# A hybrid decoder layer on one core: three buffers for pairs of experts, the ple gate weights loaded last, e scaled where it is drained, decay rows spread by bf16 matmuls

## The chip, the core and the metric

The kernel runs on one NeuronCore of a Trainium2 chip. The time is the device time of one execution in microseconds (us). Engines are named as in the profile: PE (TensorE matmuls), PEld (its weight loads), DVE (VectorE), ACT (ScalarE), POOL (GpSimd), SP (SyncE, which issues DMAs). The host does nothing but pass the arrays.

## What is computed

One decoder layer over 256 tokens of width 1024, all in float32:

```python
xn = rms_norm(h, norm_mix);  proj = xn @ w_in
# mixer 1: causal conv + silu, gated delta rule over chunks (8 heads x 128), decays exp(g_t - g_s)
# mixer 2: softmax attention with forget gates (16 heads x 64): s + c_t - c_s, causal
h = h + (sigmoid(gate_a) * y_a + sigmoid(gate_f) * y_f) @ w_out
# 64 experts, top 8, hidden 256, plus one shared expert
hn = rms_norm(h, norm_ffn)
routed = sum over e of (silu(hn @ we_gate[e]) * (hn @ we_up[e]) * gate[:, e]) @ we_down[e]
h = h + routed + (silu(hn @ ws_gate) * (hn @ ws_up)) @ ws_down
# per-layer input embedding
e = rms_norm(p @ w_ple, ple_norm)
g = sigmoid(rms_norm(h, ple_gate_norm) @ w_ple_gate)
out = h + g * e
```

The weights of the 64 experts are 3.1 MB each in float32, 201 MB in all; every other input together is some 60 MB.

## The kernel before

Each engine has its own program, and semaphores order them. The 256 tokens are two tiles of 128 (n = 0, 1). PSUM has eight banks; up to the expert loop, `bank_fills()` lists every use of a bank, which go round the eight in that order. PE waits for a bank's last reader (`open_bank`), the reader waits for the fill (`wait_filled`), and other steps wait for it to be drained (`wait_drained`). A big arena of SBUF is cut by hand, and its parts are used again in later stages.

**Mixers.** A tile of 512 columns of a weight matrix (2 MB) is projected for both token tiles by `project` (L722, eight matmuls of 128x512 in float32, which the profile shows as 16 records). Between the projections of mixer 2's columns PE fills `gb.j` and `bb.j` (L784): rows of g and beta of 16 heads and chunks, spread over all 128 partitions. For that DVE copies the transposed g and beta (`gbT`) out, POOL writes a block diagonal array from it with `affine_select` (`gd`, `bd`, 16 partitions x 2048), and PE multiplies it by ones: one float32 matmul with 16 rows and 512 columns for each j of 4 and each of the two kinds. `cb.j` (L893, eight of them) spreads the cumulated forget gates of mixer 2 in the same way, from `cd` (16 x 4096), which POOL writes once `o1.0` and `o1.1` are filled.

**Embedding.** PE computes p @ w_ple in four pieces `e.n.j` (L971). ACT copies each to `e_t` (L546). Behind the shared expert's silu ACT squares and sums `e_t` (L666, written to `hn` as a dump), then copies the transposed hidden of the shared expert (L669), on which PE's second matmul of that expert (L1028) waits. POOL makes the root. DVE scales `e_t` by the root and by `ple_norm` (L1516, L1517) in front of its expert loop; at the end it multiplies by the gate (L1557) and adds h (L1558).

**Experts.** A loop takes two experts (a pair) at a time, 32 pairs. A token tile gives each expert up to 32 slots (a second pass over all pairs would run if an expert had more; here one pass runs). For a pair PE does: gate and up products (L1075, 64 records), the adding of the former pair's output to the tokens (L1053), two transposes (L1082), the gathering of the next pair's tokens by one-hot bf16 matmuls (L1041, 48), two small ones (L1046, L1047), and the down product (L1093, 32 records). A pair's weights are 6.29 MB: gate and up 2.1 MB each, down 2.1 MB. They go to one of **two** buffers (`pair_at`, `gu_in`, `d_in`), each loaded by three DMAs on SP (`load_pair`, L408 and L411): gate and up once PE has done L1075 of the pair that had the buffer, down once PE has done its L1093. Pair 0 is loaded when the transposed mixture is drained, pair 1 when `wo.1.1` is filled, both ahead of the loop. The weights of the ple gate (`wpg`, 4.2 MB, used by L1117 behind the loop) have memory of their own and are loaded by two DMAs on ACT's queue (L678) just ahead of ACT's loop. PE's, DVE's and SP's loops have a body of two pairs.

## Time and profile before

| | |
|---|---|
| median of 3 runs | 1047.62 us (1047.4 to 1049.5) |
| profiled execution, whole | 1047.64 us |
| its span, first to last instruction | 1045.9 us |
| TensorE clock granted, mean | 0.998 |
| PE busy, share of the span | 1001.6 us, 96% |
| DVE, ACT, POOL busy | 315.3, 205.6, 61.7 us |
| moved by DMA | 264.41 MB, mean 253 GB/s |
| chain that ended last | PE 62%, DMA 32%, DVE 3% |

The profile's busy time of PE is modelled at its end, so 96% does not say that PE is never waiting. The stages by the span's time: up to 106 us convolution and its projections; to 204 the projections of mixer 2 with `gb` and `bb`; to 310 the triangular inverse; to 358 merge gates with `cb`; to 429 attention; to 530 output projection, router, shared expert; 530 to 1008 the expert loop; then the ple gate and the store.

### The profile page before, as it was taken

The page shows a single profiled execution, that of the slowest core. Times are in us where ns is not written, and L with a number is a line of the kernel's source. Part 1 is how long each engine was busy: PE and PEld are TensorE (multiplying, and loading weights), DVE is VectorE, ACT ScalarE, POOL GpSimd, SP SyncE. Part 2 cuts the span into 40 slices and gives each one's busy share as a digit, 9 for nine tenths or more (in the row PEclk, how much of TensorE's full clock was granted, in tenths as well). Part 3 has the DMA queues.
Part 4 walks back from the last instruction along what each step waited for, and adds up shares of the span by engine and source line. Part 5 has one row for each costly group of instructions (what it writes and reads, how often), then busy time and mean ns, then how long its engine had stood idle before and what let it go on. Part 6 is the DMA issues. An engine that isn't in the chain of part 4 may idle for free.

```text
span 1045.9 us, 17182 instructions
## 1 busy us (share of the span) xinstructions
PE 1001.6 (96%) x7371; PEld 519.8 (50%) x7371; DVE 315.3 (30%) x691; ACT 205.6 (20%) x407; POOL 61.7 (6%) x84
## 2 busy tenths in 40 slices
PE   6999999999999999999999999999999999999998
PEld 5888443579874555444743333333333333333343
DVE  2555802266636334112521111111111111111122
ACT  1200201215330563111301111111111111111111
POOL 5000600000052000000000000000000000000000
PEclk9999999999999999999999999999999999999999
DMA  7633342420022242656459999999999999999911
GB/s 226 236 139 138 125 161 81 161 81 1 1 81 80 81 154 88 232 186 246 190 192 414 421 421 421 421 421 421 421 420 421 420 421 421 421 421 421 421 42 41
DMA packets 60338, 264.41 MB, mean 253 GB/s; under 512 B 5921, under 2 KB 8338, under 8 KB 35346
## 3 DMA queue, kind: packets, MB, share of 16 engines
q1 hardware_dynamic: 58226, 259.77, 62.2%
q10 hardware_dynamic: 2080, 4.19, 1.1%
q8 instruction: 22, 0.36, 0.1%
q14 instruction: 10, 0.08, 0.0%
HBM read 262.91 MB, written 1.05 MB: 252 GB/s over the span
## 4 chain that ended last, share of the span: by engine, by line
PE 62%; DMA 32%; DVE 3%; ACT 1%; issue 1%; SPq 1%; POOL 0%; DVEq 0%; ACTq 0%; POOLq 0%
DMA arena<-in_we_up 31%; PE bank L722 23%; PE bank L1075 12%; PE bank L750 8%; PE bank L807 5%; PE bank L715 3%; PE bank L1117 3%; PE bank L1008 1%; ACT arena L546 1%; PE bank L1028 1%; PE bank L784 1%; PE bank L893 1%; SPq L408 1%; PE bank L874 1%; PE bank L1093 1%
## 5 line engine op out<-in xcount | busy, mean ns | idle before, releaser
L1075 PE MATMUL bank<-arena 128*32 128x512 f32 x2048 | 226.3, 593 | 17.9 <-DMA arena<-in_we_up 16.8
L722 PE MATMUL bank<-arena,actT 128*128 128x512 f32 x384 | 169.3, 596 | 0.0
L1075 PEld LDWEIGHTS bank<-arena 128*32 128x32 f32 x2048 | 69.7, 110 | 173.3 <-issue 154.4
L546 ACT ACTIVATE arena<-bank 128x512 f32<-128x512 f32 (+2 forms) x132 | 70.7, 571 | 247.0 <-PE bank L722 154.7
L722 PEld LDWEIGHTS bank<-arena,actT 128*128 128x128 f32 x384 | 71.4, 190 | 91.1 <-issue 90.3
L1093 PE MATMUL bank<-arena 128*32 128x512 f32 x1024 | 116.5, 595 | 0.0
L722 PE MATMUL bank<-arena 128*128 128x512 f32 x192 | 83.9, 595 | 2.0 <-ACT arena L546 2.0
L750 PE MATMUL bank<-actT,arena 128*128 128x256 f32 x384 | 83.8, 380 | 1.6 <-DVE actT L1156 1.6
L1526 DVE SCALAR_TENSOR_TENSOR arena<-arena,gslot,bank 128x256 f32<-128x256 f32 x32 | 15.4, 481 | 230.2 <-ACT arena L685 230.2
L750 PEld LDWEIGHTS bank<-actT,arena 128*128 128x128 f32 x384 | 72.6, 190 | 11.7 <-issue 2.0
L685 ACT ACTIVATE arena<-bank 128x256 f32<-128x256 f32 x32 | 12.3, 383 | 278.6 <-PE bank L1075 278.6
L1053 PE MATMUL bank<-arena 64*128 64x512 f32 x256 | 63.6, 615 | 0.0
L807 PE MATMUL bank<-arena 128*128 128x128 f32 x512 | 59.5, 275 | 1.3 <-ACT arena L546 1.3
L1093 PEld LDWEIGHTS bank<-arena 128*32 128x32 f32 x1024 | 30.0, 109 | 59.2 <-issue 57.4
L807 PEld LDWEIGHTS bank<-arena 128*128 128x128 f32 x512 | 58.3, 192 | 1.9 <-issue 1.9
L722 PEld LDWEIGHTS bank<-arena 128*128 128x128 f32 x192 | 36.0, 190 | 46.1 <-issue 46.1
L715 PE MATMUL bank<-ident,arena 128*128 128x128 f32 x333 | 44.4, 281 | 11.0 <-DVE arena L1145 7.4
L1041 PE MATMUL bank<-onehot,arena 128*128 128x64 bf16 x1584 | 51.6, 193 | 0.0
L1041 PEld LDWEIGHTS bank<-onehot,arena 128*128 128x128 bf16 x1584 | 50.7, 98 | 0.9 <-issue 0.6
L715 PEld LDWEIGHTS bank<-ident,arena 128*128 128x128 f32 x333 | 39.0, 145 | 20.7 <-issue 17.5
L1529 DVE COPY arena<-bank 128x512 f32<-128x512 f32 x32 | 22.1, 692 | 88.5 <-PE bank L1041 88.5
L1538 DVE COPY arena<-bank 128x512 f32<-128x512 f32 x32 | 22.1, 692 | 77.7 <-PE bank L1093 77.7
(226 smaller groups left out, 709.4 us busy)
## 6 DMA issues: line engine op xcount, KB each, us to landing
arena<-in_we_gate SPq DMA_DIRECT2D x32, 2048.0 KB, 17.4
arena<-in_we_up SPq DMA_DIRECT2D x32, 2048.0 KB, 21.9
arena<-in_we_down SPq DMA_DIRECT2D x32, 2048.0 KB, 20.2
arena<-in_w_in SPq DMA_DIRECT2D x17, 2048.0 KB, 7.6
arena<-in_w_branch_gdn SPq DMA_DIRECT2D x2, 2048.0 KB, 9.2
arena<-in_w_branch_fox SPq DMA_DIRECT2D x2, 2048.0 KB, 8.0
arena<-in_w_out SPq DMA_DIRECT2D x2, 2048.0 KB, 7.8
arena<-in_w_ple_gate ACTq DMA_DIRECT2D x2, 2048.0 KB, 22.3
```

The costliest lines, as they stand in the source:

```text
L546: a.activation(dst, ps(name)[:, 0:cols_used] if len(dst.shape) == 2 else ps(name)[:, 0:cols_used].rearrange("p (a b) -> p a b", a=dst.shap ...
L715: ins = t.transpose(o[0:w, i * P:i * P + rows_in], v, ident[0:rows_in, 0:rows_in])
L722: ins = t.matmul(o[:, :], lhs[:, c, n * P:n * P + P], w[:, c, :], start=(c == 0), stop=(c == KC - 1))
L750: ins = t.matmul(o[:, i * S:i * S + S], w[:, c, col:col + P], actT[:, c, :], start=(c == 0), stop=(c == KC - 1))
L807: ins = t.matmul(o[:, i * P:i * P + P], lhs(b), rhs(b), start=True, stop=True)
L1041: ins = t.matmul(bank[5 + half][:, c * P + n * 2 * CAP:c * P + (n + 1) * 2 * CAP], hparts[:, k, n, (4 * half + c) * P:(4 * half + c + 1) * P],
L1053: ins = t.matmul(bank[2 * n + j][:, :], spread[s][hp, :], y[hp, WT * j:WT * j + WT], start=False, stop=False, skip_group_check=True)
L1075: ins = t.matmul(bank[4][i * CAP:i * CAP + CAP, :], xg[:, c, i * CAP:i * CAP + CAP], w, start=(c == 0), stop=(c == KC - 1))
L1093: ins = t.matmul(bank[4 + j][i * CAP:i * CAP + CAP, :], hidT[:, c, i * CAP:i * CAP + CAP], d_in[s][:, i % 2, c * D + WT * j:c * D + WT * j ...
L1117: ins = t.matmul(bank[4 + NT * j + n][:, :], actT[:, c, n * P:n * P + P], wpg[j][:, c, :], start=(c == 0), stop=(c == KC - 1))
L1529: v.tensor_copy(xg[:, 4:8, :], bank[6][:, :].rearrange("p (c s) -> p c s", c=4)).then_inc(xb_ready, 1)
L1538: v.tensor_copy(y[:, WT:D], bank[5][:, :]).then_inc(y_ready[1], 1)
```

## The change

**A ring of three.** `SLOTS = 3`, `pair_at = [24576, 12288, 0]`. To fit a third buffer in the arena, other things move: the shared expert's weights and hidden, `hn`, `ple_norm` and the output tile into the down part of a buffer, `spread` into `actT`, and `wpg` into the gate and up part of buffer 2. SP's loads ahead of the loop are in another order (the `...` below `mT` is the shared expert's gate and up weights), and `wpg` is loaded by SP last, once PE has done L1075 thirty times (`passes` holds the 30 for one pass), the last time for pair 29. The loops of PE, DVE and SP have a body of three pairs; on PE and DVE the first and the last pair stand outside, on SP the last two loads.

```diff
-        pair_at = [PAIR_WORDS, 0]
+        pair_at = [24576, 12288, 0]
...
-        wpg = [at(WPG + i * KC * WT, KC * WT).rearrange("p (c n) -> p c n", c=KC) for i in range(2)]
+        wpg = [at(pair_at[2] + i * KC * WT, KC * WT).rearrange("p (c n) -> p c n", c=KC) for i in range(2)]
...
+            load_gate_up(0, slice(0, 2))
+            wait_filled(sp, "yf.1.1")
             sp.dma_start(ngain, norm_ffn.to_broadcast([P, D])).then_inc(ngain_loaded, 16)
+            for n in range(NT):
+                wait_drained(sp, f"mT.{n}.1")
...
+            load_gate_up(1, slice(2, 4))
+            wait_filled(sp, "wo.0.1")
+            load_gate_up(2, slice(4, 6))
             wait_filled(sp, "wo.1.0")
             wait_filled(sp, "wo.1.1")
+            sp.dma_start(sdw, ws_down[0].rearrange("(q c) d -> q c d", c=2)).then_inc(sdw_loaded, 16)
+            wait_filled(sp, "sh.0")
+            wait_filled(sp, "sh.1")
+            load_down(1, slice(2, 4))
+            for n in range(NT):
+                for j in range(2):
+                    wait_drained(sp, f"e.{n}.{j}")
+            sp.wait_ge(parts_ready, 2 * NT)
+            load_down(0, slice(0, 2))
+            sp.wait_ge(shared_done, 1)
+            load_down(2, slice(4, 6))
+            with sp.Fori(0, PAIRS // SLOTS - 1) as k:
+                for s in range(SLOTS):
+                    load_pair(s, bass.ds(k * 6 + (6 + 2 * s), 2), k * SLOTS + (s + 1))
+            for i in range(PAIRS // SLOTS * SLOTS, PAIRS):
+                load_pair(i % SLOTS, slice(2 * i, 2 * i + 2), i - SLOTS + 1)
...
+            sp.wait_ge(pgu_filled, sp.value_load(passes[0:1, 2:3], min_val=PAIRS - 2, max_val=PAIRS * (P // CAP) - 2))
+            for j in range(2):
+                sp.dma_start(wpg[j], w_ple_gate[0].rearrange("(c q) n -> q c n", q=P)[:, :, WT * j:WT * j + WT]).then_inc(wpg_loaded, 16)
```

**e at its drain.** ACT squares and sums `e.n.j` straight from PSUM (four of 512, each into a column of its own), DVE drains the bank as it multiplies by `ple_norm`, and the root is applied at the end in the multiplication by the gate. L666, L1516 and L1517 are gone.

```diff
-                drain(f"e.{n}.{j}", e_t[:, n, WT * j:WT * j + WT])
+                a.activation(ejunk, ps(f"e.{n}.{j}")[:, :], ACT.Square, accum_out=e_ss[:, 2 * n + j:2 * n + j + 1]).then_inc(ess, 1)
...
+                close(v.tensor_tensor(e_t[:, n, WT * j:WT * j + WT], ps(nm)[:, :], plen[:, WT * j:WT * j + WT], ALU.mult), nm)
...
-                    seq(v.tensor_tensor(o, o, e_t[:, n, WT * j:WT * j + WT], ALU.mult))
+                    seq(v.scalar_tensor_tensor(out=o, in0=e_t[:, n, WT * j:WT * j + WT], scalar=e_ri[:, n:n + 1], in1=o, op0=ALU.mult, op1=ALU.mult))
```

**Rows spread in bf16.** DVE splits g, beta and the forget sums into three bf16 parts (four small operations each time), PE transposes the 48 rows in bf16, and each head's row is spread by a bf16 matmul of 48 rows whose weights are a column of a constant `pick`, repeated 128 times. POOL's three `affine_select` and the waits on them are gone.

```diff
-                close(t.matmul(o[:, :], ones[0:16, :], src[0:16, 4 * int(j):4 * int(j) + 4, :], start=True, stop=True), name)
+                for i in range(4):
+                    ins = t.matmul(o[:, i * P:i * P + P], bc(pick[:, 4 * int(j) + i], 1, P), row, start=True, stop=True)
+                close(ins, name)
...
-                    close(t.matmul(o[:, :], ones[0:16, :], cd[0:16, 2 * j:2 * j + 2, :], start=True, stop=True), f"cb.{j}")
+                    for i in range(2):
+                        ins = t.matmul(o[:, i * S:i * S + S], bc(pick[:, 2 * j + i], 1, P), cT3, start=True, stop=True)
+                    close(ins, f"cb.{j}")
```

How the instructions stand in a row, at three places. First SP, from the last tile of w_out to the loop, before (`filled`, `drained` with a number are banks; `pgu_filled` counts L1075, `y1_filled` L1093):

```order
L378 DMA arena<-in_w_out 128x8x512 [waits filled0]
L408 DMA arena<-in_we_gate 128x2x2048 [waits drained1,drained7]
L408 DMA arena<-in_we_up 128x2x2048
L411 DMA arena<-in_we_down 128x2x2048
L417 DMA arena<-in_ws_down 128x2048
L421 DMA arena<-in_ple_norm 128x1024 [waits filled5,filled4]
L423 UNCONDITIONAL_BRANCH
L408 ISA [waits pgu_filled]
L411 DMA arena<-in_we_down 128x2x2048 [waits y1_filled]
```

and now:

```order
L383 DMA arena<-in_w_out 128x8x512 [waits filled0]
L409 DMA arena<-in_we_gate 128x2x2048
L409 DMA arena<-in_we_up 128x2x2048
L422 DMA arena<-in_norm_ffn 128x1024 [waits filled2]
L425 DMA arena<-in_ws_gate 128x2048 [waits drained1,drained7]
L426 DMA arena<-in_ws_up 128x2048
L409 DMA arena<-in_we_gate 128x2x2048 [waits filled3]
L432 DMA arena<-in_ws_down 128x2048 [waits filled5,filled4]
L412 DMA arena<-in_we_down 128x2x2048 [waits filled7,filled6]
L412 DMA arena<-in_we_down 128x2x2048 [waits drained4,drained7,parts_ready,drained6,drained5]
L412 DMA arena<-in_we_down 128x2x2048 [waits shared_done]
L444 UNCONDITIONAL_BRANCH
```

Gate and up of pair 0 now stand directly behind w_out's tile, those of pairs 1 and 2 ahead of the shared expert's down weights, and the three down loads between the shared expert and the loop.

Second, PE among the projections of mixer 2, before:

```order
L722 MATMUL bank<-arena,actT 128x512 x32
L784 MATMUL bank<-arena,ones 128x512
L722 MATMUL bank<-arena,actT 128x512 x8
...
L797 MATMUL bank<-ident,stat 16x128 x2
L715 MATMUL bank<-ident,arena 128x128 x32
```

and now (L750 is the projection, L814 the spreading, L743 the transpose `cT`):

```order
L750 MATMUL bank<-arena,actT 128x512 x32
L814 MATMUL bank<-stat,pick 128x128 x4
L750 MATMUL bank<-arena,actT 128x512 x8
...
L743 MATMUL bank<-identb,cf 48x128 x2
L737 MATMUL bank<-ident,arena 128x128 x32
```

Where one float32 matmul of 512 columns stood, four bf16 ones of 128 stand; nothing else moved there.

Third, ACT between the shared expert's silu and the expert loop, before (the rows with `shared_done` and the one behind it are the ple gate's weights):

```order
L661 ACTIVATE arena<-bank 128x256 [waits filled7]
L666 ACTIVATE arena,e_ss<-arena 128x1024 [waits drained6,drained5,parts_ready]
L666 ACTIVATE arena,e_ss<-arena 128x1024 [waits drained4,drained7]
L669 ACTIVATE arena<-bank 128x256 [waits hidT_filled] x2
L672 ACTIVATE arena<-bank 128x512 [waits xa_filled]
L678 DMA arena<-in_w_ple_gate 128x8x512 [waits e_ready,shared_done]
L678 DMA arena<-in_w_ple_gate 128x8x512
```

Now the two L666 and the two DMAs are gone from ACT, and the DMAs stand on SP behind the last pair:

```order
L460 TENSOR_LOAD passes
L460 ISA x2
L462 DMA arena<-in_w_ple_gate 128x8x512 x2
L466 DMA out<-arena 128x512 x4
```

## Rows read from the trace of the kernel before

**Rows 1.** The page's part 2: GB/s in 40 equal slices of the span

```profile
GB/s 226 236 139 138 125 161 81 161 81 1 1 81 80 81 154 88 232 186 246 190 192 414 421 421 421 421 421 421 421 420 421 420 421 421 421 421 421 421 42 41
```

**Rows 2.** The chain that ended last, in time: start us, us, what

```profile
552.93 21.58 DMA arena<-in_we_up
```

**Rows 3.** Timeline of PE in the expert loop: start, us, what, [idle before <-releaser]

```profile
530.56 7.07 PE L1075 MATMUL bank<-arena 128*32 128x512 f32 x64 [1.10 <-DVE arena L1504]
...
544.77 7.05 PE L1075 MATMUL bank<-arena 128*32 128x512 f32 x64
...
558.96 7.05 PE L1075 MATMUL bank<-arena 128*32 128x512 f32 x64
...
574.56 7.07 PE L1075 MATMUL bank<-arena 128*32 128x512 f32 x64 [1.23 <-DMA arena<-in_we_up]
...
604.46 7.07 PE L1075 MATMUL bank<-arena 128*32 128x512 f32 x64 [0.29 <-DMA arena<-in_we_up]
...
993.15 7.07 PE L1075 MATMUL bank<-arena 128*32 128x512 f32 x64 [0.29 <-DMA arena<-in_we_up]
...
1013.62 27.70 PE L1117 MATMUL bank<-arena,actT 128*128 128x512 f32 x64 [0.20 <-DVE actT L1552]
```

**Rows 4.** Busy time by stretch: PE, PEld, DVE, ACT, POOL, clock, DMA share, GB/s

```profile
510.00:535.00 25.00, 22.07 (x148) 13.11 (x150) 13.76 (x34) 3.60 (x8) 1.48 (x4) 0.93 0.00 1
...
560.00:980.00 420.00, 403.51 (x4376) 155.95 (x4372) 67.45 (x196) 54.89 (x112) 0.00 (x0) 1.00 1.01 421
```

**Rows 5.** Timelines of ACT's and SP's DMA issues around the loop's start

```profile
534.96 1.06 ACTq L678 DMA_DIRECT2D arena<-in_w_ple_gate  x2
...
537.86 0.39 SPq L408 DMA_DIRECT2D arena<-in_we_gate  x1
538.34 0.45 SPq L408 DMA_DIRECT2D arena<-in_we_up  x1
```

**Rows 6.** DMA issues from 0 to 530 us: KB each, median us to landing

```profile
arena<-in_we_up SPq DMA_DIRECT2D x2, 2048.0 KB, 13.4
```

**Rows 7.** Timeline of PE among mixer 2's projections, with gb (L784)

```profile
114.12 27.63 PE L722 MATMUL bank<-arena,actT 128*128 128x512 f32 x64
141.69 1.12 PE L784 MATMUL bank<-arena,ones 16*128 16x512 f32 x2
142.74 7.13 PE L722 MATMUL bank<-arena,actT 128*128 128x512 f32 x16
149.80 1.12 PE L784 MATMUL bank<-arena,ones 16*128 16x512 f32 x2
```

**Rows 8.** Timeline of PE among the merge gates, with cb (L893)

```profile
324.80 7.13 PE L722 MATMUL bank<-arena,actT 128*128 128x512 f32 x16
...
333.77 7.13 PE L722 MATMUL bank<-arena,actT 128*128 128x512 f32 x16
```

**Rows 9.** Timeline of PE in the first pair: the bf16 matmuls

```profile
539.75 1.56 PE L1041 MATMUL bank<-onehot,arena 128*128 128x64 bf16 x48
541.15 0.22 PE L1046 MATMUL bank<-identb,onehot 128*128 128x128 bf16 x1
...
541.31 3.64 PE L1093 MATMUL bank<-arena 128*32 128x512 f32 x32
```

**Rows 10.** Timeline of all engines from the router to the shared expert's second product

```profile
502.76 0.23 DVE L1436 TENSOR_TENSOR wsm<-wsm,rbias 128x64 f32<-128x64 f32 x1 [6.73 <-ACT wsm L546]
...
517.55 0.19 ACT L666 ACTIVATION_READ_ACCUMULATOR arena<-arena 128x1 f32 x1
...
518.19 0.29 DVE L1471 TENSOR_REDUCE gsum<-bank 128x1 f32<-128x128 f32 x1
...
519.20 8.80 PE L1028 MATMUL bank<-arena 128*128 128x512 f32 x16 [1.26 <-ACT arena L669]
```

**Rows 11.** The DMA queues from 560 to 980 us, all of them: packets, MB, share

```profile
q1 hardware_dynamic: 22833, 176.04, 100.9%
q10 hardware_dynamic: 332, 0.65, 0.4%
```

300 lines of the change are left out of this document (161 added, 139 removed).

## The prediction

> **What bounds the kernel now.** I first read the rate of the transfers over the span [rows 1]: the first half of the span moves 100 to 250 GB/s and the expert loop stands at 420 to 421 for as long as it runs. A rate that flat says that DMA is full there; the chain of waits agrees, since from 553 us on each second step of it is a load of `we_up` of 21.6 us or a little more [rows 2], 31% of the span in all. Then I read the starts of L1075 in PE's timeline [rows 3]. Pairs 0, 1 and 2 start at 530.56, 544.77 and 558.96, two steps of 14.20 us with no wait: that is PE's own time for a pair. From pair 3 (574.56) each start waits for `we_up`; from pair 3 to pair 5 (604.46) it is 29.90 us, so 14.95 us a pair, and the last, pair 31, starts at 993.15 = 574.56 + 28 x 14.95. A pair is 6.29 MB, and 6.29 MB / 14.95 us = 421 GB/s, the rate of the stretch [rows 4]. So the loop is bound by DMA, but only by 0.75 us in 15; PE's "busy" hides that. In contrast, from 510 to 535 us DMA moves 1 GB/s [rows 4]: both buffers are full, and nothing can be fetched. And the ple gate's 4.2 MB are fetched at 534.96, just in front of the first load of the loop (537.86) [rows 5], though L1117 wants them at 1013.62.
>
> **Part 1: the ring of three and the gate weights last.** Before the loop the change fetches one pair more, 14.95 us of DMA, into idle DMA time, and takes 4.2 MB (9.96 us at 421 GB/s) out of the loop's way. Together 24.9 us less lies in front of the last pair. PE can use only what brings it down to its own time. PE's floor: pair 31 starts at 530.56 + 31 x 14.20 = 970.76 instead of 993.15, which is 22.4 us earlier. DMA's floor: the loop's first load is issued at 537.86 as now (PE's first L1075 frees a buffer), but it is pair 3's. Up to the landing of pair 31's gate and up come 28 whole pairs and 9.96 us: 28 x 14.95 + 9.96 = 428.6 us, plus what a load costs beyond its bytes. For that I have two values. The two `we_up` loads ahead of the loop land 13.4 us after their issue [rows 6], some 0.48 us behind the gate's; 13.4 + 0.48 - 9.96 = 3.9. In the present loop, from the issue at 534.96 to pair 3's landing at 574.5 come 4.19 + 6.29 + 4.19 = 14.7 MB, 34.9 us, so 4.7. DMA's floor is thus 970.4 to 971.2, against 970.76 for PE: a margin of +0.4 to -0.4 us. The first pairs have slack (24.9 us at the start, which shrinks by 0.75 a pair), so it is only the last pair or two that may wait. I take 0.4 us of loss: **gain 22.0 us**. If the loop starts earlier for other reasons, both floors move with it, since the first load waits for PE.
>
> Are the earlier loads in time? Pair 0's down is now issued behind the shared expert's gate and up products (some 516 us in the old time), behind pair 1's down: two of 4.98 us and 3.9, so 530, wanted at 541.31 [rows 9]. Pair 2's down, behind L1028 (528), lands near 537, wanted 24 us later. The shared expert's down weights, wanted at 519.20 [rows 10], go out at 490 with nothing before them in the queue. Early in the loop the queue must not run dry: pair 3's 14.95 us of data begin some 2 us behind 537.86 and last to about 555; pair 4 is issued at PE's second end of L1075 (552), 1 us to spare after the same start-up. The gate weights wait for the thirtieth L1075 and stand behind pair 31's down: 971 + 4.98 + 9.96 = 986, plus nothing new for start-up; L1117 wants them at 1013.62 - 22.4 = 991. Cover of 5 us; if it is gone, each us is paid in full.
>
> **Part 2: rows spread in bf16.** Plain projections take 27.63 us for four, between starts 27.57, so 6.89 each [rows 7]. From one `gb` to the next are 149.80 - 141.69 = 8.11 us, so one costs 1.22; of that 2 of 16 records of a projection, 0.86, are columns, and 0.36 is the change of tile shape. Two `cb` with a projection take 333.77 - 324.80 = 8.97 [rows 8], so 2.08 for the two, 1.72 of columns and 0.36. PE has no gap on either side (106 to 204 us, 310 to 358), so what is saved moves everything behind it; DVE, which reads the banks, is idle most of that time. New price: 48 bf16 matmuls of 64 columns and two small ones take 541.31 - 539.75 = 1.56 us [rows 9], at most 0.0325 each, so 0.065 for 128 columns and 0.26 for the 512 of a `gb` or `cb`. Saved: 0.60 each, 16 times, **9.6 us**; I take 9.5, since the bf16 ones have their weights changed four times. The worst near row is 0.22 for a lone bf16 transpose of 128 columns [rows 9]: four of them would cost 0.88 and save nothing on the eight `gb` and `bb`, two cost 0.44 and save 0.42 on each `cb`: 3.4 us in all. The best, the columns for nothing, is 13.8. Nearest in kind is the row of 48, also a chain of different weights. The shape's 0.36 I leave, as 48 rows are still not the whole array. The two transposes `gbT` and `cT` in bf16: 0.1 us each. DVE's eight small splitting operations (0.2 us each) fall among the convolutions, where PE sets the pace; DVE is busy 30% of the span. POOL's selects ran beside PE's work: nothing.
>
> The Trainium skill ("TensorE: Matmul & The Clock Gate", section "Wait — 56ns, not 53.3ns?") gives 55.6 ns from start to start of bf16 matmuls of 128 columns at full clock. By it a `gb` costs 0.22 instead of 0.26, and part 2 would come to an estimated 10.2 us.
>
> **Part 3: e.** ACT's two L666 stood in front of L669, for which PE's L1028 waited until 519.20 [rows 10]. Without them the next that is late is DVE's L1471 (518.19 + 0.29 = 518.48), as L1028 also waits for the rank bank to be drained: gain 0.7 us. ACT's square of `e.0.0` stands in front of the four drains that PE waits for ahead of `wo`, and reading the sum adds up to 0.19 [rows 10]: loss 0.2. DVE's four new drains are 0.7 each, three of them in the 6.7 us of idle ahead of the router's 502.76 [rows 10]. The scaling that left DVE's first pair (4 us) was beside L1075: nothing. The last multiplication has the same 512 elements: nothing.
>
> **Sum.** 22.0 + 9.5 + 0.2 + 0.7 - 0.2 = 32.2 us. The profiled execution took 1047.64, 1.7 more than its span of 1045.9, and is within 0.1 of the median, so the forecast is 1047.6 - 32.2 = **1015.4 us**.
>
> **Rivals.**
> (a) *DMA stays the limit.* The floors are equal to 0.4 us, so every us of late or missing feed (the queue dry once in pairs 3 to 5, the gate's 2 KB pieces) is paid. For it: the start-up values differ by 0.8, and the reserve of the first pairs is about 1 us. Price 2 to 6 us, time 1017 to 1021.5.
> (b) *The spreading saves little*, as weights repeated from one column load slowly, or the change of shape is paid per matmul. No row of before has such weights. Price 3 to 6 us, time 1018.5 to 1021.5.
> (c) *Better than forecast*: columns nearly free and a cheaper change of shape, 1011 to 1013.5.
> (d) *Slower than before.* PE's loop body grows from two pairs to three, from 2 x 316 to 3 x 316 loads and matmuls. From 560 to 980 us only the two data queues move anything [rows 11], none for instructions, so the body of two stays in the engine through 14 turns. If the body of three did not, each of ten turns would fetch code through the full DMA engines. It decides above 32.2 / 10 = 3.2 us a turn. A load costs 3.9 us beyond its bytes (above), so with one such wait a turn the time is 1015.4 + 39 = 1054; behind a whole pair in the queue it would be 15 us a turn, 1165. Against it: the body grows by half only, and the chain shows no cost at the present turn (pair 1 to pair 2, 14.19).
> The Trainium skill ("Runtime: NRT & Kernel Launch", section "Instruction fetch mechanics") says that a taken branch out of the present window forces a fetch, which speaks against any loop; it also gives PE room for 2048 instructions, by which a body of some 950 stays, as the trace shows for 632.
> (e) *The ring is not filled*, because a moved load waits for something late: pair 2's gate and up then come 9.96 later, the time 1024.
>
> **How the numbers follow.** Forecast, 1013.5 to 1017: 0.58. (a) 0.13, (b) 0.11, (c) 0.08, (d) 0.04, (e) 0.03; something between 1025 and 1045, 0.03. From 1012 to 1021 lie the forecast, nearly all of (a) and (b) and half of (c), 0.58 + 0.12 + 0.10 + 0.04 = 0.84; a narrower range would cut into the bounds of the two start-up values and of the bf16 price. A measurement of this kernel tells about 0.2% (2 us) from no change. Faster: all but (d) and a hundredth, 0.94; same 0.02; slower 0.04.
>
> **What would show it.** In the changed trace: L1075 starts every 14.2 us to the end, with waits for `we_up` only in the last pairs, 440 us from the first to the last; 6.89 + about 0.62 from one `gb` to the next and 6.89 + about 0.88 with two `cb`; L1028 starting with DVE's release of the rank bank and no longer with L669; L1117 not waiting for its weights; DMA busy from 443 us on in pieces; no instruction packets within the loop. I am wrong in part 1 if steps of 14.95 come back from the middle on, in part 2 if a `gb` still costs 1 us, and in all if a step of PE at a turn of the loop is longer than at the others.

## The result, and the profile after

The changed kernel takes **1011.4 us** (median of 4 runs, 1011.35 to 1011.56) against 1047.9 for the kernel before (median of 4, 1047.4 to 1049.5); the ratio is 0.965, with a 95% interval of 0.963 to 0.967. The forecast was 1015.4 with a range from 1012 to 1021: the direction was right and nine tenths of the gain were foreseen (32.2 of 36.2 us, counted from the forecast's 1047.6), but the time is 4.0 us below the forecast and 0.6 us outside the range. The profiled execution took 1011.35 us with a span of 1009.6 (before: 1047.64 and 1045.9), so its span is 36.3 us shorter. All working below is on these two spans.

The page of the changed kernel first: the GB/s of the 40 slices, and the chain of waits by engine and by line.

```profile
GB/s 229 228 123 148 140 123 155 167 61 24 1 84 83 84 117 134 156 294 392 42 319 420 418 422 423 422 422 422 422 422 422 422 422 422 422 421 423 420 165 42
...
q8 instruction: 26, 0.43, 0.2%
...
PE 62%; DVE 1%; ACT 1%; issue 1%; POOL 0%; DVEq 0%; ACTq 0%
PE bank L1102 22%; PE bank L1120 11%; PE bank L750 10%; PE bank L1084 6%; PE bank L1072 5%; PE bank L1152 3%; PE bank L1039 1%; PE bank L1109 1%; PE bank L1059 1%; PE bank L983 1%; ACT arena L572 1%; PE bank L737 1%; PE bank L1002 0%; PE bank L1031 0%; PE bank L961 0%
```

DMA is still full in the loop (418 to 423 GB/s), as in [rows 1]. But it has gone from the chain, where the kernel before had a load of `we_up` in each second step [rows 2]: full and binding are two things. The timeline of PE shows which it is. Here are the first two pairs, and the last two with the product behind the loop (columns as in [rows 3]; L1102 is the old L1075, L1152 the old L1117):

```profile
516.97 7.07 PE L1102 MATMUL bank<-arena 128*32 128x512 f32 x64 [0.86 <-DVE arena L1561]
...
531.18 2.33 PE L1102 MATMUL bank<-arena 128*32 128x512 f32 x20
...
942.60 7.05 PE L1102 MATMUL bank<-arena 128*32 128x512 f32 x64
...
956.78 7.06 PE L1102 MATMUL bank<-arena 128*32 128x512 f32 x64
...
977.24 3.24 PE L1152 MATMUL bank<-arena,actT 128*128 128x512 f32 x7 [0.20 <-DVE actT L1607]
```

From pair 0 to pair 31 it is 439.81 us, 31 steps of 14.19 on average; none of the starts behind pair 0 has a wait in brackets. Before it was 462.59 [rows 3]. PE's waits from 500 us to the end, by line and releaser (total, times, longest), hold no transfer at all:

```profile
PE bank L1102 <- DVE arena L1561: 0.9, 1, 0.9
PE bank L1138 <- issue: 0.9, 1, 0.9
PE bank L1145 <- DVE h L1602: 0.7, 1, 0.7
PE bank L1059 <- DVE gsum L1527: 0.7, 1, 0.7
PE bank L1051 <- DVE arena L1519: 0.6, 1, 0.6
PE bank L1152 <- DVE actT L1607: 0.2, 1, 0.2
```

It was close, though. Here are the last pair's `we_up` and the ple gate weights in the timeline of SP's queue (start and length of the issue), and then the view of the transfers for the issues from 921 to 928 us (last column: us from issue to landing):

```profile
921.33 1.93 SPq L409 DMA_DIRECT2D arena<-in_we_gate  x1
923.30 4.62 SPq L409 DMA_DIRECT2D arena<-in_we_up  x1
...
935.52 22.84 SPq L462 DMA_DIRECT2D arena<-in_w_ple_gate  x2
```

```profile
arena<-in_we_up SPq DMA_DIRECT2D x1, 2048.0 KB, 33.2
```

923.30 + 33.2 = 956.5, and pair 31 starts at 956.78. A `we_up` that landed 13.4 us after its issue with only the gate weights ahead of it [rows 6] now takes 33 us behind a full queue and still comes 0.3 us before it is wanted. The other signs of part 1 hold too: the last instruction packets of the loop move before 600 us, and none from there to 940.

The spreading, in PE's timeline, with a `gb` (L814) and the two `cb` (L923) between projections (L750):

```profile
141.62 0.39 PE L814 MATMUL bank<-stat,pick 48*128 48x128 bf16 x4
141.95 7.13 PE L750 MATMUL bank<-arena,actT 128*128 128x512 f32 x16
149.01 0.40 PE L814 MATMUL bank<-stat,pick 48*128 48x128 bf16 x4
...
325.33 0.61 PE L923 MATMUL bank<-stat,pick 48*128 48x256 bf16 x4
325.87 7.13 PE L750 MATMUL bank<-arena,actT 128*128 128x512 f32 x16
332.94 0.61 PE L923 MATMUL bank<-stat,pick 48*128 48x256 bf16 x4
```

149.01 - 141.62 = 7.39, against 8.11 in [rows 7]; 332.94 - 325.33 = 7.61, against 8.97 in [rows 8]. So 0.72 us is saved at a `gb` and 0.68 at each `cb` of a pair. With 6.89 us for the projection, 0.50 is left for the one `gb` and 0.72 for the two `cb`.

Last, the shared experts, in PE's timeline and then PE's busy time and granted clock in slices of 2 us. This is where the unforeseen part lies. Of after:

```profile
506.26 0.63 PE L1051 MATMUL bank<-ident,arena 128*128 128x128 f32 x4 [0.58 <-DVE arena L1519]
507.54 7.11 PE L1059 MATMUL bank<-arena 128*128 128x512 f32 x16 [0.65 <-DVE gsum L1527]
```

```profile
507.00:509.00 2.00, 1.46 (x4) 1.00 0.93 393
509.00:511.00 2.00, 2.00 (x6) 1.00 0.95 401
511.00:513.00 2.00, 2.00 (x6) 1.00 1.06 446
```

And the slices of the same product in the kernel before, where L1028 began at 519.20 behind a wait of 1.26 us and took 8.80 us [rows 10]:

```profile
518.00:520.00 2.00, 0.80 (x2) 0.94 0.00 0
520.00:522.00 2.00, 2.00 (x3) 0.50 0.00 0
522.00:524.00 2.00, 2.00 (x5) 0.71 0.00 0
```

The columns are the slice, its length, PE's busy time with its count, the granted clock, DMA's share and GB/s. At a clock of 0.50, that is 1.2 instead of 2.4 GHz, the same sixteen matmul records take longer: L1028 needed 8.80 us where L1059 needs 7.11. The three slices lose 0.12 + 1.00 + 0.58 = 1.70 us of full clock, so the low stretch lasted 3.4 us. That clock was in the trace of before, and even in a row that the prediction read for its GB/s: [rows 4] gives a mean clock of 0.93 for 510 to 535 us, which is 1.75 us lost.

**Where the 36.3 us went**, by the distances between the same instructions in both traces:

| Stretch | us |
|---|---|
| spreading and its two transposes, up to the first scores | 11.57 |
| a new wait in the attention (below) | -0.44 |
| reading the sum of ACT's square, ahead of `wo` | -0.08 |
| wait ahead of L1028 / L1059 | 0.62 |
| L1028 / L1059 itself: clock | 1.70 |
| wait of the first pair for DVE | 0.23 |
| loop, pair 0 to pair 31 | 22.78 |
| behind the start of pair 31 | -0.08 |

The new wait: the first softmax of ACT and DVE comes late by a little (what it waits behind is tested below). Before, the same product (L952) had no wait. The 0.23 us in front of the first pair were not foreseen either, and no run isolates them.

```profile
357.21 0.88 PE L983 MATMUL bank<-arena 128*64 128x128 f32 x12 [0.47 <-ACT arena L572]
```

### The profile page after: what moved, and what is told of

It is laid out like the page before. It is cut to its first block, busy times and chain, and to the rows that moved or that the text cites. A ratio compares the mean times of both kernels' runs of the same rounds, so it can differ in the third digit from the quotient of the medians.

```text
span 1009.6 us, 17206 instructions
## 1 busy us (share of the span) xinstructions
PE 982.6 (97%) x7387; PEld 514.4 (51%) x7387; DVE 309.0 (31%) x700; ACT 203.9 (20%) x407; POOL 56.0 (6%) x87
## 4 chain that ended last, share of the span: by engine, by line
PE 62%; DVE 1%; ACT 1%; issue 1%; POOL 0%; DVEq 0%; ACTq 0%
PE bank L1102 22%; PE bank L1120 11%; PE bank L750 10%; PE bank L1084 6%; PE bank L1072 5%; PE bank L1152 3%; PE bank L1039 1%; PE bank L1109 1%; PE bank L1059 1%; PE bank L983 1%; ACT arena L572 1%; PE bank L737 1%; PE bank L1002 0%; PE bank L1031 0%; PE bank L961 0%
## 5 line engine op out<-in xcount | busy, mean ns | idle before, releaser
L1102 PE MATMUL bank<-arena 128*32 128x512 f32 x2048 | 225.6, 592 | 0.9 <-DVE arena L1561 0.9
L750 PE MATMUL bank<-arena,actT 128*128 128x512 f32 x384 | 169.3, 596 | 0.0
L1102 PEld LDWEIGHTS bank<-arena 128*32 128x32 f32 x2048 | 66.9, 110 | 153.1 <-issue 152.1
L572 ACT ACTIVATE arena<-bank 128x512 f32<-128x512 f32 (+2 forms) x128 | 68.4, 570 | 234.1 <-PE bank L750 146.6
L750 PEld LDWEIGHTS bank<-arena,actT 128*128 128x128 f32 x384 | 71.4, 190 | 84.9 <-issue 84.1
L750 PE MATMUL bank<-arena 128*128 128x512 f32 x192 | 83.9, 595 | 2.1 <-ACT arena L572 2.1
L1084 PE MATMUL bank<-arena,actT 64*128 64x512 f32 x256 | 63.6, 615 | 0.0
L1120 PEld LDWEIGHTS bank<-arena 128*32 128x32 f32 x1024 | 30.0, 109 | 59.2 <-issue 57.4
L750 PEld LDWEIGHTS bank<-arena 128*128 128x128 f32 x192 | 36.0, 190 | 46.2 <-issue 46.2
## 6 DMA issues: line engine op xcount, KB each, us to landing
arena<-in_w_ple_gate SPq DMA_DIRECT2D x2, 2048.0 KB, 33.2
```

The costliest lines, as they stand in the source:

```text
L572: a.activation(dst, ps(name)[:, 0:cols_used] if len(dst.shape) == 2 else ps(name)[:, 0:cols_used].rearrange("p (a b) -> p a b", a=dst.shap ...
L750: ins = t.matmul(o[:, :], lhs[:, c, n * P:n * P + P], w[:, c, :], start=(c == 0), stop=(c == KC - 1))
L1084: ins = t.matmul(bank[2 * n + j][:, :], spread[s][hp, :], y[hp, WT * j:WT * j + WT], start=False, stop=False, skip_group_check=True)
L1102: ins = t.matmul(bank[4][i * CAP:i * CAP + CAP, :], xg[:, c, i * CAP:i * CAP + CAP], w, start=(c == 0), stop=(c == KC - 1))
L1120: ins = t.matmul(bank[4 + j][i * CAP:i * CAP + CAP, :], hidT[:, c, i * CAP:i * CAP + CAP], d_in[s][:, i % 2, c * D + WT * j:c * D + WT * j ...
```

## The experiments

Most executions of one kernel lie within 4 us here, and the traces show steps that come from how fast the first matmuls of the q, k and v projection run (last section). Single executions lie further out (1017.9 of the changed kernel, 1025.1 of the turns of fifteen, 1052.3 of the kernel before); their mean clock is lower (0.996, 0.993, 0.996), and none of them has a trace. A median of four runs therefore can't tell 1 us. Beside the measured times the table gives distances within each trace, in which that part cancels: all are counted from the first matmul of the first plain projection (106.2 us in the trace of after). "Shared" is the start of the shared experts' second product (L1028, L1059), "pair 0" that of the loop, "loop" from pair 0 to pair 31, "end" the span's end. Each ratio is to runs of the kernel before on the same chip, whose median was 1047.7 to 1048.0.

| Kernel | median us | ratio, 95% interval | shared | pair 0 | loop | end |
|---|---|---|---|---|---|---|
| before | 1047.9 | 1 | 412.9 | 424.3 | 462.6 | 939.6 |
| before, bf16 spreading | 1034.7 | 0.987 (0.985 to 0.989) | 401.9 | 411.4 | 461.6 | 925.8 |
| before, gate weights last | 1040.1 | 0.992 (0.990 to 0.994) | 412.9 | 424.3 | 454.8 | 931.8 |
| before, squares behind copies | 1046.2 | 0.9985 (0.9975 to 0.9994) | 412.3 | 421.9 | 462.7 | 937.4 |
| before, spreading and padding | 1050.9 | 1.002 (1.001 to 1.004) | 417.3 | 426.8 | 461.5 | 941.0 |
| after | 1011.4 | 0.965 (0.963 to 0.967) | 401.3 | 410.7 | 439.8 | 903.4 |
| after, again | 1013.3 | 0.968 (0.965 to 0.970) | 401.3 | 410.7 | 439.8 | 903.4 |
| after, squares put back | 1013.8 | 0.967 (0.966 to 0.969) | 401.9 | 411.3 | 439.8 | 904.0 |
| after, third gate and up late | 1018.3 | 0.972 (0.970 to 0.974) | 401.5 | 410.9 | 446.4 | 910.1 |
| after, turns of fifteen pairs | 1020.3 | 0.975 (0.972 to 0.978) | 401.5 | 410.9 | 445.7 | 909.5 |
| after, turns of six pairs | 1038.7 | 0.992 (0.990 to 0.993) | 401.3 | 410.7 | 463.5 | 927.0 |
| after, `cb` early | 1012.8 | 0.967 (0.965 to 0.968) | 401.0 | 410.4 | 439.8 | 903.1 |
| after, `cb` early, pairs | 1011.6 | 0.965 (0.963 to 0.967) | 399.8 | 409.2 | 439.8 | 901.9 |
| after, fours and bank order | 1009.4 | 0.964 (0.962 to 0.965) | 399.0 | 408.5 | 439.8 | 901.1 |

### The spreading alone

The kernel before with the changed `spread_rows`, `key_decays`, `part_transposes` and the splitting on DVE, and nothing else of the change.

```
-                close(t.matmul(o[:, :], ones[0:16, :], src[0:16, 4 * int(j):4 * int(j) + 4, :], start=True, stop=True), name)
+                for i in range(4):
+                    ins = t.matmul(o[:, i * P:i * P + P], bc(pick[:, 4 * int(j) + i], 1, P), row, start=True, stop=True)
+                close(ins, name)
```

> Kernel before with the bf16 spreading alone (pick, three bf16 terms, one transpose each; ring of two, e and the ple gate weights as before). Theory from the trace after: the PE path of parts 2 is worth 0.72 us at each of the eight gb/bb places, 0.68 at each pair of key-decay tiles, 11.6 us in all up to the attention, of which a new wait of 0.44 us before the first pv product takes some back; the DMA-bound loop starts earlier by as much: 11.1 us less, about 1036.7 us. By the prediction's own sizes (16 times 0.60, and 0.2): 9.7 less, 1038.1. By the rival that the spreading saves little: 1043 to 1046.

Measured: the median is 13.0 us below before. In the traces the end comes 13.8 us earlier: 11.0 up to the shared experts, close to the theory's 11.1 and not the prediction's 9.7; then 1.8 more up to pair 0, and 1.0 in the loop. The loop is bound by DMA as before, at 422 instead of 421 GB/s; I don't know why it is that little faster. Of the 1.8, 1.7 is the clock again, and it came as a surprise, for this kernel still has the two squares and the same wait:

```profile
508.41 0.63 PE L1029 MATMUL bank<-ident,arena 128*128 128x128 f32 x4 [0.58 <-DVE arena L1481]
510.30 7.10 PE L1037 MATMUL bank<-arena 128*128 128x512 f32 x16 [1.26 <-ACT arena L669]
```

The waits are those of before (0.57 and 1.26 us), but the product takes 7.10 us and not 8.80.

### The gate weights last, alone

```
-            act.wait_ge(shared_done, 1)
-            act.wait_ge(e_ready, NT)
-            for j in range(2):
-                act.dma_start(wpg[j], ...).then_inc(wpg_loaded, 16)
...
+            sp.wait_ge(shared_done, 1)
+            sp.wait_ge(pgu_filled, PAIRS - 2)
+            for j in range(2):
+                sp.dma_start(wpg[j], ...).then_inc(wpg_loaded, 16)
```

> Kernel before with the ple gate weights fetched by SP behind the last pair's weights instead of by ACT ahead of the loop; everything else as before, the ring has two buffers. If the DMA queue sets the loop of before, the 4.19 MB leave the queue ahead of the last pair: at 421 GB/s 9.96 us less, about 1037.8 us, and L1117 still waits for no weights. If something else set the loop, or the end now waits for them: 0 to 5 us less.

Measured: 7.6 us less by the medians, 7.8 by the traces, all of it in the loop (462.6 to 454.8); L1117 waits for nothing but DVE, as before. So the loads are what sets the loop of before from pair 3 on, and the end has room for late weights. But 9.96 was expected and 2.2 us are missing. They are found at the loop's start. GB/s is the last column; first the kernel before, then this one, whose times all lie 1.9 us later:

```profile
535.00:538.00 3.00, 3.00 (x30) 0.94 (x21) 0.00 (x0) 0.31 (x1) 0.00 (x0) 1.00 0.57 161
538.00:541.00 3.00, 3.00 (x53) 1.90 (x50) 0.48 (x1) 0.80 (x3) 0.00 (x0) 1.00 1.04 401
```

```profile
537.00:540.00 3.00, 3.00 (x28) 0.95 (x22) 0.01 (x1) 0.38 (x1) 0.00 (x0) 1.00 0.00 0
540.00:543.00 3.00, 3.00 (x57) 2.00 (x54) 0.47 (x1) 0.85 (x2) 0.00 (x0) 1.00 0.68 216
```

The gate weights were issued 2.9 us before the loop's first load could be [rows 5], and began in time in which the queue was otherwise empty: (161 + 401 - 0 - 216) GB/s times 3 us is 1.0 MB, 2.5 us of the queue. A transfer removed from a full queue is worth its bytes only as far as it ran in full time. The other 15.0 us of the loop's 22.8 are the third buffer's, and the prediction's floors, which were drawn from issue to landing, have both in them.

### The shared experts and the clock

Two kernels. Before, with ACT's two copies of the shared hidden tile ahead of its two squares:

```
-                a.activation(hn[:, n, :], e_t[:, n, :], ACT.Square, accum_out=e_ss[:, n:n + 1]).then_inc(ess, 1)
             for n in range(NT):
                 act.wait_ge(hidT_filled, n + 1)
                 a.activation(shidT[n], ...).then_inc(hidT_ready, 1)
...
+                a.activation(hn[:, n, :], e_t[:, n, :], ACT.Square, accum_out=e_ss[:, n:n + 1]).then_inc(ess, 1)
```

> Kernel before with ACT's two copies of the shared experts' transposed hidden tile (L669) moved ahead of its two 1024-wide squares (L666); nothing else is changed. Theory of the clock: PE's wait ahead of L1028 falls from 1.26 us to about 0.65, the granted clock stays at 1.00 through L1028, which takes 7.1 us instead of 8.8, and the loop starts 2.3 to 2.5 us earlier: about 1045.3 us. Rival, the wait alone (the clock fell for another reason): 0.6 to 0.7 us less, 1047.0, and L1028 still takes 8.8.

After, with two such squares put back ahead of the copies:

```
+            for n in range(NT):
+                a.activation(junk16[n], h[:, n, :], ACT.Square, accum_out=unused[:, n:n + 1])
             for n in range(NT):
                 act.wait_ge(hidT_filled, n + 1)
```

> Changed kernel with two 1024-wide squares of h, whose results nothing uses, put on ACT ahead of the two copies of the shared hidden tile (L695), where the kernel before had its squares of e. Theory of the clock: PE's wait ahead of L1059 grows by about 0.6 us, the granted clock falls below 1.00 in the stretch behind it and L1059 takes 8.8 us instead of 7.1: 2.3 to 2.5 us more than 1011.4, about 1013.8. Rival, the wait alone: 0.6 to 0.7 more, 1012.1, with L1059 at 7.1.

Measured, first kernel: 2.2 us less in the trace, 1.6 by the medians (10 and 13 runs). The wait is 0.64 and ends by DVE, the product takes 7.11. Second kernel: the wait is back at 1.26, but the product still takes 7.10, and the end comes only 0.6 us later. PE's rows of the two:

```profile
518.55 7.11 PE L1028 MATMUL bank<-arena 128*128 128x512 f32 x16 [0.64 <-DVE gsum L1471]
```

```profile
508.09 0.63 PE L1055 MATMUL bank<-ident,arena 128*128 128x128 f32 x4 [0.58 <-DVE arena L1523]
509.98 7.10 PE L1063 MATMUL bank<-arena 128*128 128x512 f32 x16 [1.26 <-ACT arena L699]
```

The first alone would have looked like proof that the longer wait makes the clock fall; the second shows that it need not. So the prediction's 0.7 us for the wait was right (0.6 in both directions), and the 1.7 us of the clock comes on top in some executions only. In the kernel with the gate weights last the fall was there again, behind the same waits (the product's first slice at 0.73, the next at 0.50):

```profile
521.08 8.80 PE L1028 MATMUL bank<-arena 128*128 128x512 f32 x16 [1.26 <-ACT arena L673]
```

```profile
521.00:523.00 2.00, 1.92 (x4) 0.73 0.00 0
523.00:525.00 2.00, 2.00 (x4) 0.50 0.00 0
```

To see whether the moment of the pause decides, I put extra matmuls of `merge.0.0` into the kernel with the spreading, so that the shared experts should come at their old time:

```
+            for c in range(18):
+                t.matmul(o[:, :], actT[:, c % KC, 0:P], w[:, c % KC, :], start=(c % KC == 0), stop=(c % KC == KC - 1 or c == 17))
             project("merge.0.0", w, 0)
```

> Kernel before with the bf16 spreading, and with 18 matmuls of 0.595 us put ahead of merge.0.0 whose sums are overwritten, so that the shared experts come at nearly the time they have in the kernel before (10.7 us later than in b_spread). Theory that the fall of the granted clock at the shared experts' second products (8.8 us before, 7.1 in b_spread behind the same waits of 0.58 and 1.26 us) hangs on when the pause comes and not on how long it is: 8.8 us again, 12.4 us more than b_spread (10.7 and 1.7) when both have the same start. Rival, it hangs on something that the spreading changed: 7.1 us, 10.7 more.

Measured: 15.2 us more than with the spreading alone. I had mis-sized the padding: such a matmul is two records and costs 6.89 / 8 = 0.86 us, so eighteen are 15.5 us and not 10.7. The product came at 523.7, 4.4 us too late for the test, and ran at full speed (7.10) behind waits of 0.57 and 1.27. What is shown: in the traces the same pause leaves the clock alone in three kernels and not in two, so its length alone doesn't decide. The two that fell have no bf16 spreading, and the three that didn't have it.

The executions without a trace speak against taking that for the rule. Each has its mean granted clock on record. In every kept trace with one low stretch of 3.4 us the mean is 0.998, and in every one with none (but for the span's last microseconds) it is 0.999 or 1.000. By this mark the clock fell in 28 of 33 executions of the kernel before on three chips (one of them with 0.996), and three of the five that stayed at 0.999 or above took 1045.95 to 1046.35 us, 1.5 to 2.1 below the median of their chip. With the long wait kept, it fell in 2 of 4 with the gate weights last, in 1 of 4 with the spreading alone, in 2 of 4 with the squares put back, and in 0 of 8 with the padding. With the wait of 0.65, it fell in 2 of 10 with the squares behind the copies, and in the changed kernel in 0 of 4 and, again, 1 of 5 (the one at 1017.9). So whether the clock falls differs from one execution to the next of the same program, and a shorter wait went with fewer falls. This is a hint and not a proof, for a mean doesn't say where the clock fell. What decides in a single execution stays open.

### How much room the ring has

The gate and up weights of the third pair are issued behind the shared experts, where the queue has less time of its own.

```
-            wait_filled(sp, "wo.0.1")
-            load_gate_up(2, slice(4, 6))
...
             sp.wait_ge(shared_done, 1)
+            load_gate_up(2, slice(4, 6))
             load_down(2, slice(4, 6))
```

> Changed kernel with the gate and up weights of the third pair issued behind the shared experts (ahead of the third pair's down weights) instead of before them. 4.19 MB, 9.96 us of the queue at 421 GB/s, move into the stretch of the loop, where the trace after leaves some 3.5 us of it unused at 522 to 526. Theory that the changed loop has hardly any reserve left (the last up weights land 0.3 us before they are wanted): 6.2 us more, about 1017.6 (5.2 to 6.5 more), with PE's waits for weights in the last pairs alone. Rival, the third buffer leaves a reserve of several us in the loop: 0 more, 1011.4.

Measured: the loop takes 446.4 instead of 439.8, 6.6 us more, and the time is 1018.3. Pairs 1 to 21 start every 14.19 us; from pair 22 (829.63) on the steps are 14.3 to 15.2. The only transfer among PE's waits from 500 us on:

```profile
PE bank L1101 <- DMA arena<-in_we_up: 4.6, 9, 0.8
```

(The idle time that is put down to the loads is less than the steps lose; as PE's ends are modelled, the steps from start to start are the measure.)

9.96 us of transfer were moved behind the start of the loop. There the queue has one gap; this is the slice from 522 to 527 us, GB/s last, of after and of this kernel:

```profile
522.00:527.00 5.00, 5.00 (x59) 2.26 (x52) 0.48 (x1) 0.77 (x2) 0.00 (x0) 1.00 0.38 113
```

```profile
522.00:527.00 5.00, 5.00 (x49) 2.00 (x42) 0.48 (x1) 0.60 (x2) 0.00 (x0) 1.00 1.01 423
```

The gap took (423 - 113) GB/s times 5 us, 1.6 MB or 3.7 us of the queue. The other 6.3 us pushed the last loads out, and 6.6 us were paid: there was no reserve beyond a few tenths, as the landing of the last `we_up` had shown. This supports the prediction's picture: DMA's floor and PE's floor are equal here to well under 1 us. With two buffers and the gate weights last, the longer steps begin at pair 12.

### Does a turn of PE's loop cost something?

The prediction's rival (d) had bodies that the engine must fetch again. The body of three pairs (some 950 loads and matmuls) showed no long step. I wrote the same 30 pairs as two turns of fifteen and as five turns of six.

```
-                with pe.Fori(0, PAIRS // SLOTS) as k:
-                    for i in range(1, SLOTS + 1):
-                        s = i % SLOTS
-                        pair(s, i - 1, r * PAIRS + k * SLOTS + i, ...)
+                with pe.Fori(0, 5) as k:
+                    for i in range(1, 7):
+                        s = i % SLOTS
+                        pair(s, (i - 1) % SLOTS, r * PAIRS + k * 6 + i, ...)
```

> Changed kernel with TensorE's loop over pairs written as two turns of fifteen pairs (some 4700 instructions) instead of ten turns of three (some 950); the same operations in the same order, the other engines' loops as they were. Theory that a turn costs TensorE nothing while instructions come ahead of need: all 31 steps from pair to pair at 14.19 us, 1011.4. Rival that the jump back to code no longer held has to be waited for: one long step between the 16th and the 17th pair, by a few us (the prediction's fourth rival needed over 3.2 us a turn), 1014 or more.

> Changed kernel with TensorE's loop as five turns of six pairs (some 1900 instructions a turn, against 950 without and 4700 with a long step). If the jump back is free as long as the body is still held and 1900 are: all 31 steps 14.19 us, the time of the changed kernel. If not: four long steps, each 4.2 us and 1.7 in the step behind it as in the kernel of two turns, 24 us more, about 1035.

Measured, turns of fifteen: one step of 18.37 and one of 15.91 behind it, at the one jump back; 5.9 us in all. Turns of six: a long step of 18.2 to 18.3 at each of four jumps, 23.7 us in the loop, and a median of 1038.7 (the profiled execution, 1036.7, is the fastest of the four, and the others have a lower mean clock). So bodies of 1900 and 4700 cost, and one of 950 doesn't. From the turns of fifteen, PE's row at the jump and the slices with the granted clock (last but two):

```profile
751.82 8.77 PE L1102 MATMUL bank<-arena 128*32 128x512 f32 x64 [4.00 <-issue]
```

```profile
752.00:754.00 2.00, 2.00 (x16) 0.58 (x12) 0.00 (x0) 0.00 (x0) 0.00 (x0) 0.74 1.02 426
754.00:756.00 2.00, 2.00 (x16) 0.75 (x12) 0.00 (x0) 0.00 (x0) 0.00 (x0) 0.50 1.02 414
```

From the turns of six, the page's instruction queue and PE's waits:

```profile
q8 instruction: 65, 1.06, 0.4%
```

```profile
PE bank L1102 <- issue: 15.6, 4, 3.9
```

PE stands for 3.9 us at each jump, "issue", that is for nothing of the program's, and 65 packets of instructions are fetched instead of 26 (eight from 606 to 690 us, which is about one turn). Then the clock may fall: the four jumps cost 4.0, 5.8, 6.9 and 7.0 us in two steps each, so 0 to 3 us come from the clock behind equal pauses. The prediction's price for one wait of this kind, 3.9 us a turn, is the pause that was measured; that it was taken from what a load of weights costs beyond its bytes makes the match partly luck. With the clock it is 6. Ten turns have nine jumps back, and at that price they would have made the change slower than before (an estimate of 1011 + 9 x 5.9 = 1064).

The Trainium skill ("Runtime: NRT & Kernel Launch", section "Instruction fetch mechanics") says that a taken branch to code outside the present window must wait for a fetch; these two kernels agree, with 3.9 us. The same section gives PE room for 2048 instructions, and the body of about 1900 loads and matmuls was not held; waits and register work come on top and are not counted here. No run here places the limit between 950 and 1900.

### What a place costs, and a better kernel

First the new wait in the attention: `cb.6` and `cb.7` ahead of `merge.2.0`, so that DVE's six copies of them are out of the way.

```
-    f += ["cb.5", "merge.2.0", "cb.6", "cb.7"]
+    f += ["cb.5", "cb.6", "cb.7", "merge.2.0"]
```

> Changed kernel with the last two key-decay tiles (cb.6, cb.7) spread ahead of the product merge.2.0 instead of behind it. Theory: VectorE's six copies of them (2.0 us) leave the chain to the first softmax, the wait of 0.47 us before the first pv product goes, and one change between bf16 and fp32 work (0.28 us) with it: 0.7 us less than 1011.4, about 1010.7. If the wait ends by another step: 0.3 less, 1011.1.

Then the `gb` and `bb` tiles two at a place:

```
-              (2, 0): ["gb.0"], (2, 1): ["gb.1"], (3, 0): ["gb.2"], (3, 1): ["gb.3"],
+              (2, 1): ["gb.0", "gb.1"], (3, 1): ["gb.2", "gb.3"],
```

> As the kernel with cb.6 and cb.7 early, and the eight tiles gb and bb spread two at a place (four places) instead of one at a place (eight). Theory that a place costs 0.28 us whatever its columns: four places fewer, 1.1 us less again, 1.8 less than 1011.4 in all, about 1009.6. Rival, the cost goes with the matmuls and not with the places: as the kernel with cb.6 and cb.7 early alone; slower if VectorE, which gets the first tile 7.2 us later, comes late at cT.

Measured: 0.3 us less in the trace for the first, where 0.7 was expected, and 1.5 for both (0.3 and 1.2), where 1.8 was. The wait before the first pv product is gone:

```profile
357.17 0.88 PE L982 MATMUL bank<-arena 128*64 128x128 f32 x12
```

but no place was saved: the next projection behind the small score products starts where it did (242.0 us from the reference point, 241.9 before), so `cb.6` and `cb.7` cost as much ahead of `merge.2.0` as behind it. That the wait went shows that DVE's copies of these two tiles, filled just ahead of the scores, had held up the first softmax. At the eight places between projections, in contrast, each of the four removed gives back 0.3 us. So the 0.28 us is the price of leaving and coming back to the fp32 projections. The medians of the two, on one chip, differ by 1.2 us, too, which alone would show little.

Last, the four `gb` at one place and the four `bb` at another, and the shared experts' product into the bank of the ranks last:

```
+            for n, j in ((0, 1), (1, 0), (1, 1), (0, 0)):
+                pe.wait_ge(hidT_ready, n + 1)
+                if n + j == 0:
+                    wait_drained(pe, "rank")
```

> The changed kernel itself, as the control of the next one on the same chip. Between 1011.4 and 1014.5 us; the runs differ by how long the first matmuls of the projection of q, k and v run at half speed (steps of 1.9 and 3.3 us seen between traces); from the first matmul of the loop over pairs to the first of the last pair 439.8.

> Changed kernel with cb.6 and cb.7 early, the four gb tiles spread at one place and the four bb tiles at another (two places instead of eight), and of the shared experts' products the one into the bank that the ranks still hold issued last. From the runs before: the early cb tiles 0.3 us less, a place 0.32 us each, six places fewer 1.9, the wait of 0.65 ahead of L1059 down to about 0.2, 0.4 less: 2.6 us less than the changed kernel on this chip. Rival: VectorE or ScalarE, which get all four gb tiles 14 us later, come late at the key and query products, and 1 to 3 us go back: 0 to 1.5 less.

Measured: the control repeats every distance of the changed kernel (table); its five runs lie from 1011.45 to 1017.9, median 1013.3, one above the range given. The new kernel: 2.3 us less in the trace (2.6 expected), 1009.4 against 1013.3 by the medians; part of those 3.9 us is the start. The wait in front of the shared experts' product is 0.35 instead of 0.65 and ends by ACT's copy:

```profile
505.57 7.11 PE L1058 MATMUL bank<-arena 128*128 128x512 f32 x16 [0.35 <-ACT arena L695]
```

DVE got its four `gb` tiles later and had time for it; no wait of PE grew. This kernel is faster than the changed one, by 2.3 us in 1011; the interval of its ratio (0.962 to 0.965) ends where that of the control (0.965 to 0.970) begins.

## Why the prediction was near, and outside its range

Of the spans' 36.3 us, 32.2 were foreseen. The 4.10 between them are 0.78 of the loop, 1.87 of the spreading less 0.44 of a new wait, 1.70 of the clock, and 0.19 of small ones. The mechanisms held; two steps failed. Part 2 sized its matmuls and the change of shape too high (9.7 us where 11.57 came). And part 3 gave the shorter wait ahead of L1028 its price, but left the product behind it at its 8.80 us: a change of the clock stood in the sum as nothing, without a reason, and was 1.7 us. Either alone would have left the time inside the range.

**Part 1, the loop: 22.0 foreseen, 22.78 measured.** The mechanism was right in each piece: PE's own pace to the end, both floors equal, the queue never dry, the gate weights in time. 0.4 us were taken off for waits in the last pairs that did not come (the last load landed 0.3 us early; with floors as near as this, which side of zero it fell was luck). The rest is rounding: 31 steps were put at 14.20, and they are 14.187.

**Part 2, the spreading: 9.7 foreseen, 11.57 measured**, of which 0.44 was lost again in the attention. This is a term of the sum that was mis-sized, in both its pieces. The 512 columns were put at 0.26 and take 0.22; the change of tile shape was kept at 0.36 ("as 48 rows are still not the whole array") and is 0.28. That is 0.12 us more at each of eight `gb` and `bb` and 0.08 at each of eight `cb`, 1.6 in all; the rest of the 1.9 is the 0.1 that was rounded off and what the transposes gave beyond 0.2. The nearest row, 48 matmuls of 64 columns in 1.56 us, was a bound from above: doubled for 128 columns it gives 0.065, and 0.055 was measured. The sentence on the Trainium skill stood beside it ("TensorE: Matmul & The Clock Gate", section "Wait — 56ns, not 53.3ns?", 55.6 ns for 128 columns): two tiles of `cb` against one tile of `gb`, four matmuls each, differ by 0.72 - 0.50 = 0.22 for four times 128 columns, 55 ns each, so the trace agrees, and the estimate of 10.2 us made with it was nearer.

That the attention would get a wait was not foreseen. The part asked whether DVE reads the banks in time, and didn't follow what DVE and ACT do behind the last tile before PE needs them.

**Part 3, e: 0.5 foreseen, 0.54 measured** for the waits (0.62 and -0.08), by the releaser that was named (`gsum`). Putting the squares back cost 0.6. What it left out is the next point.

**Missing from the sum: 1.7 us of clock.** The prediction quoted the 8.80 us of L1028 and didn't ask why sixteen records of this shape took 8.80 when every other such group takes 7.1. The page's clock of 40 slices is too coarse to show it, but the 0.93 of [rows 4] does, and slices of 2 us show 0.50. With that seen, a gain of 0 to 1.7 us would have stood as a bound below the forecast, and the range would have begun at 1010. Without this term the time would have been 1013.1, inside it. The fall itself has no shown cause: the shorter wait may have made it rarer, but it also failed to come behind the long one.

**The rivals.** (c), 1011 to 1013.5, held the result, for the reason it gave (cheaper columns and a cheaper change of shape) as to 1.6 us of the 4.0; most of the rest was the clock, of which it says nothing, and that is luck. (a) was one step away: the floors are as equal as it said, and moving 9.96 us of transfer behind the start of the loop made it true, at 6.6 us. (b), (d) and (e) did not happen; (d) is a real mechanism with a real price, and the body of three pairs is on the right side of it.

**The slower rival** was rightly held unlikely for one reason, the row that showed no instruction packets in the loop of two. The other argument, "the body grows by half only", was none: double the body of after, and the change loses two thirds of its gain in the trace, and three quarters by the medians. Its threshold of 3.2 us a turn counted ten jumps where there are nine.

## What to carry to other kernels

Before a group's duration goes into a sum, compare it with other groups of the same shape, and read the clock column beside the GB/s; a longer one hides a clock or a wait that a change may move. A single trace shows one execution: look at the mean clock of the others before you call a difference in clock the kernel's. A loop that is bound by transfers by a few per cent needs its two floors worked out to the last landing, and a transfer taken from its front is worth only what it took of full time. And when a loop's body is unrolled further, look for one step per turn that is longer than the others, released by "issue".

## What the runs showed of the hardware

- **Granted clock behind a pause.** Pauses of 0.57 and 1.26 us were followed by a clock of 0.50 (1.2 GHz) for 3.4 us in the traces of two kernels and by none in three; pauses of 3.9 us at a loop's jump were followed by 0, 1.7, 2.8 and 2.9 us of loss. By the mean clocks on record it differs between executions of one kernel, too. The length of the pause alone doesn't tell.
- **The start.** The first plain projection starts at 106.2 to 109.7 us in the traces, in steps of about 1.9 and 1.5 us, with the same program ahead of it. It is in the q, k and v projection: these are its first matmuls to 24 us, in the trace of after and in that of the turns of fifteen.

```profile
12.59 11.68 PE L778 MATMUL bank<-actT,arena 128*128 128x256 f32 x53 [1.58 <-DVE actT L1191]
```

```profile
13.09 11.19 PE L778 MATMUL bank<-actT,arena 128*128 128x256 f32 x37 [1.58 <-DVE actT L1191]
```

  53 records against 37 in about the same time. PE's slices of 4 us from 16 us on follow, of after and then of the turns of fifteen; from 20 us on both have 20 records in 4 us.

```profile
16.00:20.00 4.00, 4.00 (x20) 1.00 0.37 89
```

```profile
16.00:20.00 4.00, 4.00 (x12) 1.00 0.17 21
```

  The column says 1.00 in both, but in the second it is no measurement: the clock record kept with each trace begins with a stretch of full clock, at 10.7 to 11.5 us in the seven traces that start at 106.2 to 106.5, at 15.9 to 16.8 in the five around 108.1 (107.95 to 108.4), and at 19.0 and 19.1 in the two of 109.5 and 109.7. Ahead of it nothing is recorded, and the column counts that as full. From 14 to 18 us the turns of fifteen have 6 records of this shape in 2 us and after has 11. So the start is told by when the engine comes to full clock, and that differs from one execution to the next with the same program.
- **SP's issue of a transfer.** 0.37 to 0.45 us in the loop of the kernel before [rows 5], and 0.37 to 0.42 in the loop of after up to 815 us, while the loads land within 28.8 us of their issue. From 822 us on, when `we_up` lands 29.5 to 33.2 us behind its issue, that issue takes 2.1 to 4.6 us, and the last two loads of after take 22.84 together (15.65 in the kernel of two buffers with the gate weights last). So it goes with how much is queued and not with the number of buffers. It costs nothing here, as SP has only this to do.
- **A jump back of TensorE's loop**: nothing for a body of some 950 loads and matmuls, 3.9 us for one of 1900 and 4.0 for one of 4700, while DMA was full.
